# Two more four-unit up pairs in each feed-forward network, with the work of ScalarE and VectorE at the heads put in another order

## The reference, cut to what matters

```
def swiglu(h, w_gate, w_up, w_down):
    return (jax.nn.silu(h @ w_gate) * (h @ w_up)) @ w_down
...
x = x + 0.5 * swiglu(rmsnorm(x, ffn1_norm), ffn1_w_gate, ffn1_w_up, ffn1_w_down)
x = x + mixer(rmsnorm(x, mix_norm))                 # latent attention and HGRN2, one w_in, one w_out
x = x + cross_attention(rmsnorm(x, xattn_norm), rmsnorm(mem, mem_norm))
x = x + 0.5 * swiglu(rmsnorm(x, ffn2_norm), ffn2_w_gate, ffn2_w_up, ffn2_w_down)
```

## Time and profile before

| | before |
|---|---|
| median of 3 runs | 1871.99 us (1871.69 to 1872.52) |
| the profiled execution: its time | 1871.54 us |
| the profiled execution: its span | 1869.7 us |
| TensorE busy | 1863.0 us, 100% of the span |
| VectorE busy | 1644.3 us, 88% |
| ScalarE busy | 1123.1 us, 60% |
| DMA, mean share of 16 engines | 58% |

### The profile page before, as it was taken

The page is one execution under the profiler, slowest core; times in us unless marked ns, Lnnn a source line. Parts: engine busy times, 40 slices in busy tenths (PEclk is TensorE's granted clock), DMA queues, the critical chain, the costliest instruction groups (busy, mean ns, idle before and its releaser), DMA issues.

```text
span 1869.7 us, 23347 instructions
## 1 busy us (share of the span) xinstructions
PE 1863.0 (100%) x8760; PEld 1562.1 (84%) x8760; DVE 1644.3 (88%) x2043; ACT 1123.1 (60%) x1498; POOL 96.2 (5%) x98
## 2 busy tenths in 40 slices
PE   9999999999999999999999999999999999999999
PEld 8788888888889888988888888888888888888987
DVE  6999999999999978787676774689999999999997
ACT  7676665656666547556476655666665655656654
POOL 0000000000000002312260000000000000000000
PEclk9999999999999999999999999999999999999999
DMA  9665655756566574456443554456565656565654
GB/s 342 223 216 178 208 187 202 259 179 199 174 199 220 209 242 148 145 172 223 137 156 113 208 190 142 157 170 214 169 209 185 236 185 217 196 201 186 203 197 158
DMA packets 175009, 362.57 MB, mean 194 GB/s; under 512 B 8880, under 2 KB 20144, under 8 KB 174256
## 3 DMA queue, kind: packets, MB, share of 16 engines
q1 hardware_dynamic: 174464, 360.89, 57.7%
q10 hardware_dynamic: 432, 0.19, 0.0%
HBM read 358.95 MB, written 2.10 MB: 193 GB/s over the span
## 4 chain that ended last, share of the span: by engine, by line
PE 54%; DVE 0%; issue 0%; ACT 0%; POOL 0%; DVEq 0%
PE acc L2140 9%; PE acc L2142 9%; PE acc L2141 9%; PE acc L2129 6%; PE acc L2131 5%; PE acc L2130 5%; PE small L2142 1%; PE small L2140 1%; PE small L2141 1%; PE tr L2088 1%; PE small L2356 1%; PE tr L2142 1%; PE tr L2141 1%; PE tr L2140 1%; PE tr L2156 1%; PE small L2548 0%
## 5 line engine op out<-in xcount | busy, mean ns | idle before, releaser
L1388 DVE TENSOR_TENSOR w_lo<-w_raw,w_hi 128x1024 fp32r<-128x1024 f32 (+3 forms) x768 | 798.7, 1077 | 25.8 <-ACT w_hi L768 8.0
L779 ACT ACTIVATE w_hi<-w_raw 128x1024 fp32r<-128x1024 f32 (+3 forms) x416 | 386.8, 966 | 71.1 <-PE acc L2142 48.4
L2140 PE MATMUL acc<-w_hi,hT_hi 128*128 128x512 f32 (+1 forms) x912 | 352.2, 386 | 1.0 <-DVE w_lo L1388 1.0
L2142 PE MATMUL acc<-w_lo,hT_hi 128*128 128x512 f32 (+1 forms) x912 | 350.1, 384 | 0.0
L2141 PE MATMUL acc<-w_hi,hT_lo 128*128 128x512 f32 (+1 forms) x912 | 350.0, 384 | 0.0
L885 ACT ACTIVATE w_hi<-w_raw 128x1024 fp32r<-128x1024 f32 (+1 forms) x224 | 230.7, 1044 | 120.1 <-DVE w_raw L1398 87.0
L878 ACT ACTIVATE w_hi<-w_raw 128x512 fp32r<-128x512 f32 (+1 forms) x224 | 183.2, 834 | 141.0 <-PE acc L2142 138.0
L1320 DVE TENSOR_TENSOR w_lo<-w_raw,w_hi 128x1024 fp32r<-128x1024 f32 (+1 forms) x166 | 197.1, 1229 | 24.6 <-ACT w_hi L779 23.0
L2140 PEld LDWEIGHTS acc<-w_hi,hT_hi 128*128 128x128 f32 x912 | 171.2, 188 | 33.8 <-DVE w_lo L1388 2.5
L2142 PEld LDWEIGHTS acc<-w_lo,hT_hi 128*128 128x128 f32 x912 | 171.2, 188 | 32.5
L2141 PEld LDWEIGHTS acc<-w_hi,hT_lo 128*128 128x128 f32 x912 | 171.3, 188 | 31.3
(11 more groups left out here) (354 smaller groups left out, 2850.2 us busy)
## 6 DMA issues: line engine op xcount, KB each, us to landing
w_raw<-in_ffn_w_down SPq DMA_DIRECT2D x52, 1024.0 KB, 5.3
w_raw<-in_ffn_w_gate SPq DMA_DIRECT2D x98, 512.0 KB, 3.8
w_raw<-in_ffn_w_up SPq DMA_DIRECT2D x34, 1024.0 KB, 5.1
w_raw<-in_ffn_w_up SPq DMA_DIRECT2D x62, 512.0 KB, 4.8
w_raw<-in_w_in SPq DMA_DIRECT2D x29, 1024.0 KB, 5.2
w_raw<-in_ffn_w_down SPq DMA_DIRECT2D x24, 768.0 KB, 4.5
w_raw<-in_ffn_w_gate SPq DMA_DIRECT2D x22, 768.0 KB, 4.3
w_raw<-in_ffn_w_up SPq DMA_DIRECT2D x22, 768.0 KB, 5.5
```

The source lines that it names most:

```text
L779: nc.scalar.activation(piece(w_hi, c % SPLIT, k0, k1, width), piece(raw, c % RAW, k0, k1, width), ACT.Copy).then_inc(hi_done, 1)
L1388: return v.tensor_tensor(piece(w_lo, c % RAW, k0, k1, width), piece(raw, c % RAW, k0, k1, width), piece(w_hi, c % SPLIT, k0, k1, width).bi ...
L2140: mm(dst, lhs_hi, wh, start=first, stop=False, skip_group_check=goes_on)
L2142: return mm(dst, lhs_hi, wl, start=False, stop=last, skip_group_check=goes_on)
```

## The change

Pairs (0,1) and (1,0) of both networks take UP4 in place of UP3. The fourth unit of the first pair needs the fourth token sums at once, so `token_sums`, `sums_hi` and `sums_lo` make all four in the opening, where the fourth stood in the first pair before; TensorE waits for all four ahead of each unit. On ScalarE the sums' high parts and the last slot of the opening (c + 7) stand ahead of `square_sums` in the first network. On VectorE the low parts of the first plain slot of the first pair (`plain_lo`) stand directly behind L1498 and ahead of the next `first_sums`, and a wait on VectorE's own semaphore moves behind it.

```diff
-        FOUR = [(0, 2), (0, 4), (1, 1), (1, 3)]
+        FOUR = [(0, 1), (0, 2), (0, 4), (1, 0), (1, 1), (1, 3)]
...
-                        if m == m0 and (kind, n) == ("p", 0):
-                            sums_hi(sums_before(f) + H_SUMS - 1, [(hS_hi[:, H_SUMS - 1], hS_sum[:, H_SUMS - 1])])
...
+                for n in range(H_SUMS):
+                    sums_hi(sums_before(f) + n, [(hS_hi[:, n], hS_sum[:, n])])
+                hi(c + 7, 0, 4, NW)
                 if f == 1:
                     act.wait_ge(x_in, 16 * TT)
                     square_sums("x1", x)
-                for n in range(H_SUMS - 1):
-                    sums_hi(sums_before(f) + n, [(hS_hi[:, n], hS_sum[:, n])])
-                hi(c + 7, 0, 4, NW)
...
-                            if t == TT - 1:
-                                done(ins)
-                        done.wait()
-                        dve.sem_inc(acc_taken[1 - GB[f]], 1)
+                        ins.then_inc(acc_taken[1 - GB[f]], 1)
+                        plain_lo(d.firsts[0], d.plains[0][1], w)
+                        dve.wait_ge(acc_taken[1 - GB[f]], (b0 + 1) // 2 + 1)
                         dve.sem_inc(ev("nat_done"), 1)
                         first_sums(d.raws[1], w)
...
-                        plain_lo(d.firsts[n - 1], d.plains[n - 1][1], w)
-                        if n == 1 and m == m0:
-                            i = H_SUMS - 1
-                            token_sums(hS_sum[:, i, 0, :], [hS_sum[:, i, k, :] for k in range(1, 4)], flat[i])
+                        if m > m0 or n > 1:
+                            plain_lo(d.firsts[n - 1], d.plains[n - 1][1], w)
...
-                        if n == 2 and m == m0:
-                            i = H_SUMS - 1
-                            sums_lo(sums_before(f) + i, [(hS_lo[:, i], hS_sum[:, i], hS_hi[:, i])])
...
-                        for n in range(H_SUMS - 1):
+                        for n in range(H_SUMS):
                             token_sums(hS_sum[:, n, 0, :], [hS_sum[:, n, i, :] for i in range(1, 4)], flat[n])
...
-                        for n in range(H_SUMS - 1):
+                        for n in range(H_SUMS):
                             sums_lo(sums_before(f) + n, [(hS_lo[:, n], hS_sum[:, n], hS_hi[:, n])])
...
-                pe.wait_ge(ev("sums_split"), sums_before(d.f) + max(n + 1, H_SUMS - 1) if d.up else sums_number(m, n) + 1)
+                pe.wait_ge(ev("sums_split"), sums_before(d.f) + H_SUMS if d.up else sums_number(m, n) + 1)
```

## The result

The changed kernel takes 1875.45 us (median; 1875.03 to 1875.89), the kernel before 1871.49 us beside it (1870.85 to 1872.52): ratio 1.0021, 95% interval 1.0014 to 1.0028. The forecast was 1875.0. The profiled execution has a span of 1873.9 us where the one before has 1869.7, 4.2 us more, and this is what the traces have to explain.

What follows compares the result with a forecast made beforehand. TensorE was taken to bound the kernel, with VectorE nearly level in the up pairs. Waits 1.5 + 1.5 + 1.0 + 1.7 = 5.7 less 2.7 of matmuls gave +3.0 us, 1875.0 with 0.45 added for the median; range 1869.7 to 1878.0.

Steps and rivals of the forecast that it cites:

- Matmuls, -2.7: Four changed pairs: each fourth unit saves 3 matmuls, 0.68 us; 12 matmuls, 2.7 us less in all.
- Pair (0,2), 1.5 in each network: Behind four-unit (0,1), VectorE needs 43.43 us against TensorE's 41.8, so TensorE waits 1.5 us in each network.
- The first pair, second network, +1.0: Pair (0,1), second network: VectorE reaches the third plain slot at 1254.2, TensorE at 1253.3; TensorE waits 1.0 us.
- the high part of the second unit can only be made when TensorE has left the first: Second network's first pair: high part not before 1237.5, holding VectorE's first split to 1238.2 instead of 1237.2, 1.0 us more.
- The first pair, first network, +1.7: Pair (0,1), first network: ScalarE's new order makes silu 1.7 us later, at 47.1; TensorE waits 1.7 us more.
- The lower bound: First network's first pair: if only ScalarE's longer order counted, silu comes at 45.9 and the term is 0.5, not 1.7.
- Pairs (1,0) and (1,1), nothing: No cost: (1,0) has 5.8 us of VectorE free, 0.5 after the change; (1,1) could start 2 us later without harm.
- Token sums in the opening, nothing: Opening: the fourth lot costs VectorE 1.06 + 0.6 and ScalarE 0.5 us where both wait today, so nothing.
- slack: Rival: VectorE's gaps at a pair's start swallow the waits; half swallowed gives 1872.2 us, all 1869.3. Chance 0.2.
- (1,1) never grew: Rival that the debt reaches (1,1): it waits up to 1.5 us in both networks, 1878.0 us. Chance 0.13.
- (0,2) waited for the whole 1.5 us: Rival, faster: VectorE not late in (0,2), the 1.12 us wait gone and the full 2.7 gained, 1868.2 us. Chance 0.05.
- The drain behind the table load: Rule weighed: a drain of about 1.38 us added to the table load makes silu 1.4 later, 1876.4 us. Chance 0.01.

Runs made afterwards that it cites:

- e13_three_in_row: Changed kernel with squares of x1 first, three units at (0,1), four at (0,2), (0,4), (1,0), (1,1), (1,2), (1,3): 1874.56 us.
- e5_mem_early: Changed kernel with the two 1 MB mem loads moved on SyncE from behind the first pair's later slots to behind its plain slots: 1874.41 us.
- e4_squares_first: Changed kernel with ScalarE's squares of x1 again ahead of the token sums' high parts and slot c+7 in the first network's opening: 1874.03 us.
- e8_three_squares_first: Changed kernel with squares of x1 first and three units at (0,1) of both networks; four-unit (1,0) and early token sums stay: 1868.86 us.
- e2_first_pair_three: Changed kernel with the first pair (0,1) of both networks back at three units, reordered head and four-unit (1,0) kept: 1870.17 us.

## Why the prediction was right, and where it was not

The total was right to 0.45 us, the change and its terms less so. Forecast was +3.0; measured are +4.0 in the medians and +4.2 in the spans. The forecast had added 0.45 because the median of three runs of the kernel before lay that much above its profiled run. Over sixteen runs beside the changed kernel that median is 1871.49, not 1871.99: half a microsecond of the closeness is this. In the order of the prediction:

*Matmuls, -2.7.* Right: 12 fewer; (1,0) at 40.8 in both networks.

*Pair (0,2), 1.5 in each network.* Right in the second: 43.3 us. The sum from two stretches of VectorE's timeline, 43.43, came within 0.15 of what the pair lasts, and e13_three_in_row shows the same 43.3 at four other places, (1,2) and (1,3) of both networks. In the first network the term was 0.9 too small. The step that I left out is the one on SyncE: with a fourth unit, the mem loads stand ahead of a weight that the pair still needs, and I had not followed the queue. e5_mem_early takes this part away (44.2 to 43.3).

*The first pair, second network, +1.0.* Wrong in size: the pair lasts 41.9, waits of 0.1. The failed step is "the high part of the second unit can only be made when TensorE has left the first". ScalarE made a 128x512 high part already here:

```profile
1237.76 0.62 ACT L878 ACTIVATE w_hi<-w_raw 128x512 fp32r<-128x512 f32 x1
```

1.3 us after the pair began at 1236.5, where I had it 4.9 us after the start. By the count that it waits for, its slot is free as soon as the first product has been made, not the whole unit. VectorE's first split of that unit shows that nothing held it:

```profile
1241.03 0.69 DVE L1386 TENSOR_TENSOR w_lo<-w_raw,w_hi 128x512 fp32r<-128x512 f32 x1
```

The pair begins 3.9 us later than in the kernel before, so the forecast's 1237.2 without the delay is 1241.1 here, and its 1238.2 with it is 1242.1. Without the delay the forecast's own sum gives 1253.2 against TensorE's 1253.3, that is, no wait.

*The first pair, first network, +1.7.* Right in mechanism. The pair lasts 44.9 from a start at 50.8, and its end has moved by 1.4, with 0.7 of matmuls gone: 2.1 of waits. Forecast was 1.7, with an end 1.0 later. Squares, rsq, table load and silu came in the forecast's order; silu at 47.68 and not 47.1, since the squares ended 0.2 later and GpSimd's rsq took from 44.98 to 46.32, 1.34 us for the 0.98 of the earlier trace rows. VectorE's product came at 54.24 for the forecast's 53.8. Undoing the order gives 1.4 us (e4_squares_first), and with three units 1.9 us of the pair (44.6 to 42.7). The lower bound, where the table load would not wait, is ruled out.

*Pairs (1,0) and (1,1), nothing.* Right: 40.8 and 41.8 in every trace with four units at both. The margin was wider than forecast, 1.9 us of VectorE free in (1,0) and not 0.5.

*Token sums in the opening, nothing.* Right: in e8_three_squares_first and e2_first_pair_three the second network's pair stays at 42.5, and the stretch ahead of it that holds its opening, (1,4) to (0,1), at the 678.3 us of the kernel before.

*What I did not foresee:* 0.9 us in the mixer. Without it and the mem loads the total would have been 1873.7. Term by term the change was missed by 1.3 us: the second network's first term was 0.9 too high, and against it stand two of 0.9 that I had not seen and 0.4 too little for the first network's first pair. That the total is off by 0.45 alone is luck: the term that was not there and the baseline both stood against the ones that were too small.

*What would show it.* I expected the listed waits for L1386 to grow to 4 to 6 us. They stayed at 1.2: of the 1.5 us in the second network's (0,2) only 0.25 are listed (43.30 less 43.05 busy). The lengths of the pairs were the right sign, the list of waits the wrong one.

*The rivals.* None came true. Only the second network's first term was missing, and that by a step that was wrong, not by slack; (1,1) never grew; and (0,2) waited for the whole 1.5 us. The drain behind the table load, weighed at 0.01, did not show either: now that the load stands behind a wait it ends at 46.38 + 1.28 = 47.66, and silu starts at 47.68.

For the mixer there is a rule as well. The Trainium skill, SBUF — State Buffer, section Who interferes with whom: a VectorE instruction with two SBUF inputs and a GpSimd instruction that reads SBUF exclude each other for a whole instruction, and the one that was issued first wins. These traces agree: GpSimd's instruction takes 1.07 us where it began 0.35 us ahead of VectorE's, and VectorE's then 1.79 for 1.23; where the two began together GpSimd's takes 2.15.

*How sure.* Shown by experiment: the neighbours' price, the late silu, the mem loads, GpSimd's part in the mixer. Only matched, not tried: that the stream's position makes the 0.35 us. Read from one trace, with no run that undoes it: why the second network's first pair does not wait. The start of the first pair (50.0 to 51.0 us over the traces) is spread that none of the kernels explains.

## What to carry to other kernels

Where two engines are level, the price of an optimisation depends on its neighbours: sum the helping engine's work from one tightest point to the next, over two tiles in a row, and place the costly form only behind a tile in which that engine has time left. Look at how long each tile lasts, since a list of waits hides those that are shorter than the overlap of the records. When a step grows, follow every queue that its loads stand in: what was moved ahead of a late load costs as much as the engine work. And undo the parts of a change one by one: here the four units at (1,0) were worth keeping for 0.7 us a network, and the other order at the head of the first pair gained only once the squares stood first again (the first pair ended at 95.2 before that and at 93.3 after, 94.2 with the old head).

## What the runs showed of the hardware that I had not expected

- The same 128x1024 GpSimd instruction took 1.07 us where it began ahead of VectorE's and 2.15 us where they began together; VectorE's took 1.79 us and 1.23. Which of the two came about went with 0.35 us in VectorE's start.
- VectorE idled for 0.48 us and not 0.13 ahead of one instruction whenever it was the 1215th record of its stream, in eight traces of eight, and in none of six others.
- 1.5 us of waiting in a pair left only 0.25 us in the list of waits.
